# The first down block's low parts in a new order on VectorE, a hold on GpSimd's sums, and five products of zeros ahead of the first projection

## The chip, the cores and the metric

The kernel runs on one core of a Trainium2 chip. The metric is the device time of one execution in microseconds, from the first instruction to the last. Four engines compute: TensorE multiplies matrices into the eight banks of PSUM, VectorE and ScalarE read and write both SBUF and PSUM, and GpSimd works on SBUF alone. SyncE issues most DMAs. Each engine takes its own instructions strictly in the order in which they are written, and engines wait for one another by semaphores that count up.

## The reference

Two layers of a decoder trunk over 1024 tokens of width 1024. Layer 0 mixes tokens with gated linear attention and an RG-LRU, layer 1 with a gated delta rule. Each layer then attends to 256 memory tokens and applies an MLP. All in float32:

```python
for i in range(DEPTH):                      # DEPTH = 2
    hn = rms_norm(h, mix_pre_g[i])
    m = gla_lru_mixer(hn, ...) if i % 2 == 0 else gdn_mixer(hn, ...)
    h = h + rms_norm(m, mix_post_g[i])
    c = mem_cross_attn(rms_norm(h, xa_pre_g[i]), rms_norm(mem, xa_mem_g[i]), xa_w_q[i], xa_w_kv[i], xa_w_o[i])
    h = h + rms_norm(c, xa_post_g[i])
    f = sq_relu_mlp(rms_norm(h, mlp_pre_g[i]), mlp_w1[i], mlp_w2[i])
    h = h + rms_norm(f, mlp_post_g[i])

def sq_relu_mlp(h, w1, w2):                 # w1 1024 x 4096, w2 4096 x 1024
    return jnp.square(jax.nn.relu(h @ w1)) @ w2
```

## The kernel before

**Three products for one.** Every float32 operand of a matrix product is split into a high part (a copy rounded to fp32r, made by ScalarE) and a low part (the operand minus its high part, made by VectorE with one subtraction), and a product is three TensorE products of 128x128 by 128x512: high x high, high x low, low x high. Weights stream through four slots: SyncE loads a 128x1024 tile into `wraw`, ScalarE writes `whi`, VectorE writes `wlo` over `wraw`.

**The start.** The first projection of layer 0 (`first_pair`, L3397) multiplies the first two weight blocks with the eight tiles of x in the order in which they arrive. For each tile ScalarE makes the high part and squares x; VectorE makes the low part and adds the squares up. Ahead of the last tile stand two plain fp32 products with a matrix of ones (`first_stat`, L3415), which sum the squares over the partitions for the RMS norm. GpSimd sets two constant columns (L1093, L1094) and counts `cols_set`; ScalarE waits for both. GpSimd then spends the projection on sums of layer-1 weights (`presum`, L1099 to L1102), which SyncE loads and stores in a ring, between loads of weight tiles.

**The MLP by Strassen products.** Up and down projection use seven products instead of eight for 2x2 blocks (in Winograd's form). In the down projection the hidden units come in seven groups (`for i in range(MLP_G - 1)`), and in each group there are four output blocks a, b, c, d with seven products each. A product such as `a6` is one instruction group on TensorE: six products of 128x512, two k-tiles with three terms each. TensorE's order is

```python
PRODUCTS = ("a1 a5 b1 b5 a2 b2 a6 a3 b6 a7 b3 a4 b7 c1 c5 b4 c6 c2 c3 c7 d1 d5 c4 d6 d2 d7 d3 d4").split()
```

Products 1, 2 and 4 of a block take weight quarters as they are, products 3, 5, 6 and 7 take sums of them: S1 to S4 are made by GpSimd (`weight_sums`, L1045 to L1059, four 128x256 sums, S1 in place, counted by `x_sum`), the high parts `xh` of S2, S4 and S3 by ScalarE (`sums_hi`), their low parts `xl` by VectorE (`sums_lo`, `part_of_sums_lo`, counted by `x_split`). The hidden operands are B11, B21, B22, T1, T2, T3, T4. For group 0 they come back from DRAM raw, so ScalarE makes their high part (`raw_hi`, L1546) and VectorE their low part (`raw_lo`, L2578). The last hidden tile is staged for the later groups at the same time: GpSimd makes T's sums (`hidden_sums`, L1036 to L1042), ScalarE high parts (`part_hi`), VectorE low parts (`part_lo`, L2522), and SyncE stores them.

**Who waits for whom in group 0 of the down projection.** Products 1, 6, 7, 4 of a block accumulate in the same bank, and each partial sum is read out before the next product adds to it. So a7 waits until a6 was read, and a4 until a7 was read. In group 0, the products 1, 5, 6, 4 of a and b are read by ScalarE (`first_copy`, L1593, counted by `lam_exp`); VectorE stands in its order with a 128x1 memset that waits for this copy (L2615). All other products are read by VectorE: a copy (L2624) or an addition into `work` (L2626). `evac` counts them in order. ScalarE's order there, in the code of `mlp`:

```python
raw_hi("T4")
part_hi(PAIRS + 1, "T4")
first_copy("b5")
down_hi(0, 2)          # block c: whi (L1508), two high parts of sums (L1514)
first_copy("a6")
first_copy("b6")
```

The copy of b5 waits for the staged low part of B21. GpSimd's order is: hidden sums of the last tile, `down_prep(0, 2)` (block c), `down_prep(0, 3)` (block d), then the blocks of group 1. `down_prep(0, 2)` waits for its weights and for an up product; `down_prep(0, 3)` for the stores of the last staged tile. VectorE's order is written out by hand in L2628 to L2653: the low parts ahead of the loop, and inside it, behind the k-th read-out, further low parts and `down_lo(i, j)`, which splits a block and its sums.

Of the kernel before, what the change touches and what calls it, by code (L numbers as in the profile page):

```python
# [25 lines left out]
P = 128  # L26
# [11 lines left out]
LRU_C = 8.0  # L38
GLA_GATE_NORM = 16.0
GLA_RANK = 16  # L40
GDN_H = 8
XA_H = 4
XA_T = 2
# [272 lines left out]
def build(nc, xT, memT, wstream, lru_w, gk_w2, pvec_in, consts_in, masks_in, outT):  # L316
# [4 lines left out]
    with ExitStack() as ctx:  # L321
# [91 lines left out]
        def bank(b, n=1):  # L413
            return flat(ps[:, b:b + n, :])
# [175 lines left out]
        def all_out(op, layer, hp):  # L590

            return out_of_op(op), 16 * (len(EARLY) if op in EARLY else len(STAGED) - len(EARLY)) * (HIDDEN * layer + hp)
# [383 lines left out]
        def _(pool):  # L976
# [48 lines left out]
            def mlp(layer):  # L1025
# [18 lines left out]
                def weight_sums(blocks, parts, x):  # L1044

                    for n in blocks:
                        pool.wait_ge(w_in[plan.slot[n]], 16 * plan.nth[n])
                    a11, a12, a21, a22 = parts
                    w = x["w"]

                    def shaped(ap):
                        return pairs_of(ap) if w < HALF else ap
                    s2, s4, s3 = shaped(x["raw24"][:, 0:w]), shaped(x["raw24"][:, w:2 * w]), shaped(x["raw3"][:])
                    k3 = link.mark(tt(s3, a11, a21, ALU.subtract))  # L1054
                    tt(a21, a21, a22, ALU.add).then_inc(x_sum, 1)  # L1055
                    link.wait(k3)
                    k2 = link.mark(tt(s2, a22, s3, ALU.subtract))
                    link.wait(k2)
                    tt(s4, a12, s2, ALU.subtract).then_inc(x_sum, 1)  # L1059
# [4 lines left out]
                def down_prep(i, j):  # L1064
                    if i == 0 and j in (0, 2):
                        pool.wait_ge(unit_done, up_unit(layer, PAIRS - 2 + j // 2, "3") + 1)
                    if i == 0 and j == 3:
                        pool.wait_ge(*all_out("T2", layer, HIDDEN))
                    weight_sums((plan.at[f"mlp{layer}.d"][0] + MLP_T * i + j,), quarters(layer, None, i, j), sums_of(None, j))

                for hp in range(PAIRS):
# [18 lines left out]
                ppool[g].credit(pool)  # L1090
            gpool.credit(pool)
            gprep.credit(pool)
            nc.gpsimd.memset(one_col, 1.0).then_inc(cols_set, 1)  # L1093
            nc.gpsimd.memset(eps_col, EPS).then_inc(cols_set, 1)  # L1094
            for h in range(PRESUMS):
# [44 lines left out]
        def _(eng):  # L1140
# [970 lines left out]
            for s in (gexp, gqd, gev, gout, *pact, *fact, *oact):  # L2111
                s.credit(eng)
            eng.wait_ge(cols_in, 16)
            eng.wait_ge(cols_set, 2)
            first_part(0, False)
            for n in range(2):
                first_hi(n, 0)
# [22 lines left out]
        def _(eng):  # L2140
# [314 lines left out]
            def mlp(layer):  # L2455
# [171 lines left out]

                for i in range(MLP_G - 1):  # L2628
                    if i == 0:
                        part_of_sums_lo(prep_no(layer, None, 0, 1), sums_of(None, 1), 0, "24")  # L2630
                        raw_lo("B21")
                        raw_lo("T2")
                        raw_lo("B22")
                        part_lo(PAIRS + 1, "B21")
                        raw_lo("T3")
                        part_of_sums_lo(prep_no(layer, None, 0, 1), sums_of(None, 1), 1, "3")
                        part_lo(PAIRS + 1, "T13")
                    eng.wait_ge(evac, down_unit(layer, i, "a1"))
                    for k in range(len(PRODUCTS)):
                        add(i, k)  # L2640
                        if i == 0 and k == 3:
                            part_lo(PAIRS + 1, "T2")
                        if i == 0 and k == 5:
                            part_lo(PAIRS + 1, "T4")
                            raw_lo("T4")
                        if k == (5 if i else 9):
                            down_lo(i, 2)
                        if k == 14:
                            down_lo(i, 3)
                        if k == 19:  # L2650
                            down_lo(i + 1, 0)
                        if k == 23:
                            down_lo(i + 1, 1)  # L2653
# [691 lines left out]
        def _(eng):  # L3345
# [36 lines left out]
            def both_halves(n, u, i=0):  # L3382
# [11 lines left out]
                                      stop=kt == KT - 1 and (hl, xp) == terms[-1])  # L3394
                last.then_inc(unit_done, 1)

            def first_pair(n, u):  # L3397

                for kt in range(KT):
                    eng.wait_ge(act_ready, kt + 1)  # L3400
                    for j in range(2):
                        if kt in (0, KT // 2):
                            eng.wait_ge(w_split if kt else w_first_split, n + j + 1)
                        for hl, xp in ((0, 0), (0, 1), (1, 0)):
                            for e in range(2):
                                last = mm(out_of(u + j)[:, E[e]],
                                          (wlo if hl else whi)[plan.slot[n + j]][:, kt * P:(kt + 1) * P],
                                          act[:, kt, xp, E[e]], start=kt == hl == xp == 0,
                                          stop=kt == KT - 1 and hl == 1)
                        if kt == KT - 1:  # L3410
                            last.then_inc(unit_done, 1)
                    if kt == KT - 2:
                        first_stat()
# [806 lines left out]
```

## Time and profile before

| | us |
|---|---|
| median of 3 runs | 2982.55 (2981.35 to 2983.25) |
| the profiled execution | 2981.7 |
| its span | 2979.9 |
| TensorE busy, share | 98% |
| VectorE / ScalarE / GpSimd busy, share | 71% / 48% / 28% |
| granted clock, mean | 0.997 |

Shares are of the span. A matmul record shows a duration longer than its spacing, since products are pipelined: the spacing of starts is the measure. Layer 0's first down group begins near 1012 us, layer 1's some 1031 us later.

### The profile page before, as it was taken

How to read it: one execution, taken by the hardware profiler on the slowest of the kernel's cores; microseconds unless marked ns; L12 is line 12 of the kernel's file. 1: busy time of each engine (PE TensorE's matmuls, PEld its weight loads, DVE VectorE, ACT ScalarE, POOL GpSimd, SP SyncE). 2: the span in 40 equal slices, each digit the busy share in tenths (PEclk: the TensorE clock that was granted, in tenths of full speed). 3: DMA queues.
4: the chain of work that ended last, by engine and by line, in shares of the span. 5: the costliest groups of instructions: out<-in, count | busy, mean ns of one | idle time of the engine just before them, and what ended most of it. 6: DMA issues, size and time to landing. Idle time of an engine off the chain costs nothing.

```text
span 2979.9 us, 44588 instructions
## 1 busy us (share of the span) xinstructions
PE 2921.5 (98%) x16844; PEld 2403.1 (81%) x16844; DVE 2116.1 (71%) x2903; ACT 1441.4 (48%) x2651; POOL 840.6 (28%) x808
## 2 busy tenths in 40 slices
PE   8999999999999999999999999999999999999999
PEld 7788888887888778887788788878888788877887
DVE  8276638647788977778977666644764778897776
ACT  4435645336777712235433566644534677762222
POOL 4629300000566633330000112200000056663333
PEclk9999999999999999999999999999999999999999
DMA  6720341003566786533444323123101356677653
GB/s 216 254 92 22 108 126 50 29 29 113 205 254 249 272 327 247 212 114 131 154 146 149 104 61 121 49 71 113 43 29 34 136 201 249 250 296 289 254 205 135
DMA packets 198593, 457.35 MB, mean 153 GB/s; under 512 B 13808, under 2 KB 71440, under 8 KB 196496
## 3 DMA queue, kind: packets, MB, share of 16 engines
q1 hardware_dynamic: 159152, 414.34, 38.9%
q10 hardware_dynamic: 39264, 40.64, 4.0%
q8 instruction: 113, 1.85, 0.3%
q14 instruction: 64, 0.52, 0.1%
HBM read 304.97 MB, written 149.95 MB: 153 GB/s over the span
## 4 chain that ended last, share of the span: by engine, by line
PE 79%; DVE 12%; ACT 3%; issue 2%; DMA 2%; POOL 1%; SPq 0%; ACTq 0%; DVEq 0%; POOLq 0%
PE ps L3375 21%; PE ps L3607 10%; PE ps L3608 10%; PE ps L3609 10%; PE ps L3847 3%; PE ps L3848 3%; PE ps L3849 3%; PE ps L3882 2%; PE ps L3449 1%; DVE work L2177 1%; PE ps L3776 1%; PE ps L3392 1%; PE ps L4013 1%; DVE hres L2208 1%; PE ps L3996 1%
## 5 line engine op out<-in xcount | busy, mean ns | idle before, releaser
L3375 PE MATMUL ps<-act,whi 128*128 128x512 f32 x2384 | 747.8, 395 | 4.1 <-DVE act L2198 2.6
L3375 PEld LDWEIGHTS ps<-act,whi 128*128 128x128 f32 x2384 | 444.1, 188 | 110.6 <-issue 12.7
L3375 PE MATMUL ps<-act,wlo 128*128 128x512 f32 x1192 | 464.5, 390 | 0.0
L2161 DVE TENSOR_TENSOR wlo<-wraw,whi 128x1024 fp32r<-128x1024 f32 x253 | 319.1, 1263 | 188.6 <-ACT whi L1156 158.8
L1036 POOL TENSOR_TENSOR stagedf<-quads 128x1024 f32<-128x1024 f32 x28 | 73.8, 2635 | 1047.3 <-ACTq L1447 1047.3
L2626 DVE TENSOR_TENSOR work<-work,ps 128x512 f32<-128x512 f32 x360 | 239.6, 684 | 127.8 <-PE ps L3609 124.7
L1508 ACT ACTIVATE whi<-wraw 128x1024 fp32r<-128x1024 f32 x112 | 115.9, 1056 | 369.1 <-POOL wraw L1055 307.5
L3375 PEld LDWEIGHTS ps<-act,wlo 128*128 128x128 f32 x1192 | 223.7, 188 | 47.1
L3607 PE MATMUL ps<-act,whi 128*128 128x512 f32 x624 | 244.7, 392 | 7.1 <-DVE work L2626 4.0
L3609 PE MATMUL ps<-act,wlo 128*128 128x512 f32 x624 | 243.0, 389 | 0.0
L1156 ACT ACTIVATE whi<-wraw 128x1024 fp32r<-128x1024 f32 x124 | 130.4, 1057 | 151.6 <-DMA wraw<-wstream_dram 148.5
L3392 PE MATMUL ps<-act,whi 128*128 128x512 f32 x608 | 161.6, 392 | 0.9 <-DVE work L2960 0.8
L3608 PE MATMUL ps<-hresr,whi 128*128 128x512 f32 x416 | 161.9, 389 | 0.0
L3608 PE MATMUL ps<-act,whi 128*128 128x512 f32 x416 | 161.9, 389 | 0.0
L3607 PEld LDWEIGHTS ps<-act,whi 128*128 128x128 f32 x624 | 117.1, 188 | 37.4 <-DVE work L2626 9.6
L3609 PEld LDWEIGHTS ps<-act,wlo 128*128 128x128 f32 x624 | 117.1, 188 | 24.7
L3392 PEld LDWEIGHTS ps<-act,whi 128*128 128x128 f32 x608 | 114.8, 189 | 25.8 <-issue 2.1
L1054 POOL TENSOR_TENSOR xr_d<-wraw 128x256 f32<-128x256 f32 x56 | 50.8, 907 | 291.9 <-DMA wraw<-wstream_dram 276.3
L2522 DVE TENSOR_TENSOR staged<-stagedf,staged 128x512 fp32r<-128x512 f32 (+1 forms) x72 | 123.1, 1758 | 3.8 <-ACT staged L1471 3.5
L2238 DVE SCALAR_TENSOR_TENSOR work<-work,pvec 128x1023 f32<-128x1023 f32 (+2 forms) x84 | 111.9, 1332 | 3.0
L2177 DVE TENSOR_TENSOR work<-work,sq 128x512 f32<-128x512 f32 x83 | 57.3, 690 | 69.4 <-ACT sq L1184 69.2
L1126 POOL MEMSET work<- 128x1024 f32 x2 | 1.8, 952 | 358.4 <-PE ps L3849 358.4
(451 smaller groups left out, 7156.4 us busy)
## 6 DMA issues: line engine op xcount, KB each, us to landing
wraw<-wstream_dram SPq DMA_DIRECT2D x248, 512.0 KB, 3.6
hid_store<-staged SPq DMA_DIRECT2D x168, 512.0 KB, 3.3
act<-hid_store SPq DMA_DIRECT2D x36, 1024.0 KB, 10.8
hresr<-hid_store SPq DMA_DIRECT2D x56, 512.0 KB, 9.9
qkvz<-work ACTq DMA_DIRECT2D x32, 512.0 KB, 2.7
work<-qkvz ACTq DMA_DIRECT2D x64, 256.0 KB, 3.1
act<-hid_store SPq DMA_DIRECT2D x30, 512.0 KB, 10.9
presum<-wstream_dram SPq DMA_DIRECT2D x48, 256.0 KB, 4.0
```

What stands on the lines that cost most here:

```text
L1156: A(whi[s][:], wraw[s][:], ACT.Copy).then_inc(w_hi, 1)
L1508: A(whi[s][:], wraw[s][:], ACT.Copy).then_inc(w_hi, 1)
L2161: TT(wlo[s][:], wraw[s][:], whi[s][:].bitcast(F32), ALU.subtract).then_inc(w_split, 1)
L2238: ins = STT(out=out[:, back:], in0=x[:, 0:SEQ - back], scalar=w(3 - back), in1=out[:, back:], op0=ALU.mult, op1=ALU.add)
L2522: TT(stage_part(op, 1), src, stage_part(op, 0).bitcast(F32), ALU.subtract).then_inc(hid_ready, 1)
L2626: TT(uh(t, e), uh(t, e), out_of(uk), ALU.add).then_inc(evac, 1)
L3375: last = mm(out_of(u)[:, 0:width], (wlo if hl else whi)[s][:, at:at + P], rhs(kt, xp, e), start=kt == hl == xp == 0, stop=kt == kts - 1 an ...
L3392: last = mm(out_of(u)[:, E[e]], (wlo if hl else whi)[s][:, kt * P:(kt + 1) * P], act[:, kt, xp, E[e]], start=kt == hl == xp == 0, stop=kt ...
L3607: mm(out, wh, xh, start=first, stop=False, skip_group_check=more)
L3608: mm(out, wh, xl, start=False, stop=False, skip_group_check=more)
L3609: return mm(out, wl, xh, start=False, stop=end, skip_group_check=more)
L3847: mm(out_of(u), wh, xh, start=first, stop=False, skip_group_check=more)
```

## The change

Three edits.

1. GpSimd clears `sq` (128x512) ahead of the two columns, and TensorE multiplies its zeros five times, as fp32 products of 128x128 by 128x512 into bank 7, ahead of the first weight product. ScalarE's wait on `cols_set` goes up by one.
2. In group 0 of both layers' down projections VectorE's low parts are put in another order, and the next group's first block is split after the 17th read-out instead of the 19th.
3. GpSimd's sums of block c in group 0 wait until `x_split` says that VectorE has made both low parts of block b's sums.

```diff
@@ LRU_C = 8.0
+WARM = 5
@@ down_prep(i, j), GpSimd
                     if i == 0 and j == 3:
                         pool.wait_ge(*all_out("T2", layer, HIDDEN))
+                    if i == 0 and j == 2:
+                        pool.wait_ge(x_split, 2 * prep_no(layer, None, 0, 1) + 2)
                     weight_sums((plan.at[f"mlp{layer}.d"][0] + MLP_T * i + j,), quarters(layer, None, i, j), sums_of(None, j))
@@ GpSimd, start
+            nc.gpsimd.memset(sq[:], 0.0).then_inc(cols_set, 1)
             nc.gpsimd.memset(one_col, 1.0).then_inc(cols_set, 1)
@@ ScalarE, start
-            eng.wait_ge(cols_set, 2)
+            eng.wait_ge(cols_set, 3)
@@ VectorE, down projection
                     if i == 0:
-                        part_of_sums_lo(prep_no(layer, None, 0, 1), sums_of(None, 1), 0, "24")
                         raw_lo("B21")
                         raw_lo("T2")
                         raw_lo("B22")
+                        sums_lo(prep_no(layer, None, 0, 1), sums_of(None, 1))
+                        raw_lo("T3")
                         part_lo(PAIRS + 1, "B21")
-                        raw_lo("T3")
-                        part_of_sums_lo(prep_no(layer, None, 0, 1), sums_of(None, 1), 1, "3")
-                        part_lo(PAIRS + 1, "T13")
+                        raw_lo("T4")
                     eng.wait_ge(evac, down_unit(layer, i, "a1"))
                     for k in range(len(PRODUCTS)):
                         add(i, k)
                         if i == 0 and k == 3:
+                            part_lo(PAIRS + 1, "T13")
+                        if i == 0 and k == 5:
                             part_lo(PAIRS + 1, "T2")
-                        if i == 0 and k == 5:
                             part_lo(PAIRS + 1, "T4")
-                            raw_lo("T4")
                         if k == (5 if i else 9):
                             down_lo(i, 2)
                         if k == 14:
                             down_lo(i, 3)
-                        if k == 19:
+                        if k == (19 if i else 17):
                             down_lo(i + 1, 0)
@@ TensorE, start
+            def zeros():
+
+                eng.wait_ge(cols_set, 1)
+                for _ in range(WARM):
+                    mm(bank(7), sq[:, 0:P], sq[:], start=True, stop=True)
+
             def first_pair(n, u):
 
+                zeros()
```

VectorE at the head of layer 0's down projection, in the kernel before. `act` and `hresr` written by L2578 are the low parts of the hidden operands, in turn B21, T2, B22 and T3; `xl24_d1` and `xl3_d1` are the low parts of block b's sums; `staged` are the stored parts; `work` is where products are read out to:

```order
L2544 TENSOR_TENSOR xl24_d1_117<-xr24_d1_115,xh24_d1_113 128x512
L2578 TENSOR_TENSOR act_51<-act_51 128x2x512
L2578 TENSOR_TENSOR hresr_74<-hresr_74,tx_79 128x2x512
L2578 TENSOR_TENSOR act_51<-act_51 128x2x512
L2522 TENSOR_TENSOR staged1_82<-quads_80,staged1_82 128x512
L2578 TENSOR_TENSOR hresr_74<-hresr_74,act_51 128x2x512
L2544 TENSOR_TENSOR xl3_d1_118<-xr3_d1_116,xh3_d1_114 128x256
L2522 TENSOR_TENSOR staged0_81<-stagedf0_83,staged0_81 128x2x512
L2615 MEMSET small_67 128x1 x4
L2522 TENSOR_TENSOR staged1_82<-stagedf1_84,staged1_82 128x512
L2626 TENSOR_TENSOR work_69<-work_69,ps 128x512 x2
L2522 TENSOR_TENSOR staged1_82<-stagedf1_84,staged1_82 128x512
```

The same place in the changed kernel, where lines stand 4 further down:

```order
L2582 TENSOR_TENSOR act_51<-act_51 128x2x512
L2582 TENSOR_TENSOR hresr_74<-hresr_74,tx_79 128x2x512
L2582 TENSOR_TENSOR act_51<-act_51 128x2x512
L2548 TENSOR_TENSOR xl24_d1_117<-xr24_d1_115,xh24_d1_113 128x512
L2548 TENSOR_TENSOR xl3_d1_118<-xr3_d1_116,xh3_d1_114 128x256
L2582 TENSOR_TENSOR hresr_74<-hresr_74,act_51 128x2x512
L2526 TENSOR_TENSOR staged1_82<-quads_80,staged1_82 128x512
L2582 TENSOR_TENSOR hresr_74<-hresr_74,act_51 128x2x512
L2619 MEMSET small_67 128x1 x4
L2526 TENSOR_TENSOR staged0_81<-stagedf0_83,staged0_81 128x2x512
L2630 TENSOR_TENSOR work_69<-work_69,ps 128x512 x2
L2526 TENSOR_TENSOR staged1_82<-stagedf1_84,staged1_82 128x512 x2
```

The first part of block b's sums has moved behind B22, the second stands with it, T3 comes ahead of B21's staged part, and T4's low part, which was next behind the rows of the kernel before, has moved ahead of the memsets. The read-outs that follow (memset of a6, addition of a3, memset of b6, addition of a7) are the same in both.

VectorE further down in the same group, in the kernel before: the memset stands for b4, the copy reads c6, the three additions c2, c3 and c7, then the next group's first block (`wlo0`, `xl24_d0`, `xl3_d0`), then four copies of which the first reads d1:

```order
L2615 MEMSET small_67 128x1
L2624 COPY work_69<-ps 128x512
L2626 TENSOR_TENSOR work_69<-work_69,ps 128x512 x3
L2161 TENSOR_TENSOR wlo0_60<-wraw0_56,whi0_52 128x1024
L2544 TENSOR_TENSOR xl24_d0_111<-xr24_d0_109,xh24_d0_107 128x512
L2544 TENSOR_TENSOR xl3_d0_112<-xr3_d0_110,xh3_d0_108 128x256
L2624 COPY work_69<-ps 128x512 x4
```

And in the changed kernel:

```order
L2619 MEMSET small_67 128x1
L2628 COPY work_69<-ps 128x512
L2630 TENSOR_TENSOR work_69<-work_69,ps 128x512
L2165 TENSOR_TENSOR wlo0_60<-wraw0_56,whi0_52 128x1024
L2548 TENSOR_TENSOR xl24_d0_111<-xr24_d0_109,xh24_d0_107 128x512
L2548 TENSOR_TENSOR xl3_d0_112<-xr3_d0_110,xh3_d0_108 128x256
L2630 TENSOR_TENSOR work_69<-work_69,ps 128x512 x2
L2628 COPY work_69<-ps 128x512 x4
```

The three instructions of the next block stand ahead of the additions of c3 and c7. ScalarE's order is the same as before, GpSimd's too but for the memset, and SyncE's is the same.

## Rows read from the trace of the kernel before

**Rows 1.** The page, busy time of the engines.
```profile
PE 2921.5 (98%) x16844; PEld 2403.1 (81%) x16844; DVE 2116.1 (71%) x2903; ACT 1441.4 (48%) x2651; POOL 840.6 (28%) x808
```

**Rows 2.** Waits of TensorE: total us, times, longest.
```profile
PE ps L3607 <- DVE xl_d L2544: 3.6, 2, 1.8
...
PE ps L3607 <- DVE act L2578: 3.1, 2, 1.6
...
PE ps L3607 <- DVE work L2624: 1.8, 2, 1.1
```

**Rows 3.** Timeline of TensorE, layer 0's first down group: start, us, instruction, idle before.
```profile
1019.14 0.47 PE L3607 MATMUL ps<-act,whi 128*128 128x512 f32 x1 [1.55 <-DVE act L2578]
...
1026.67 0.50 PE L3607 MATMUL ps<-tx,xh_d 128*128 128x512 f32 x1 [1.81 <-DVE xl_d L2544]
...
1032.81 0.50 PE L3607 MATMUL ps<-act,whi 128*128 128x512 f32 x1 [1.76 <-DVE work L2626]
...
1050.52 0.47 PE L3607 MATMUL ps<-tx,xh_d 128*128 128x512 f32 x1 [1.10 <-DVE work L2624]
```

**Rows 4.** GpSimd's groups by form: busy us, mean ns, idle before.
```profile
L1105 POOL MEMSET lin<- 128x512 f32 x3 | 1.5, 528 | 43.8 <-DVE work L2811 43.8
```

**Rows 5.** Timeline of GpSimd at the start.
```profile
1.05 0.10 POOL L1093 MEMSET pvec<- 128x1 f32 x1 [0.60 <-POOLq L4211]
```

**Rows 6.** Timeline of TensorE at the start.
```profile
8.58 2.04 PE L3406 MATMUL ps<-act,whi 128*128 128x512 f32 x4 [8.58 <-DVE wlo L3314]
...
15.58 1.07 PE L3406 MATMUL ps<-act,whi 128*128 128x512 f32 x4
...
30.54 1.88 PE L3420 MATMUL ps<-work,consts 128*128 128x512 f32 x4
```

**Rows 7.** Windows: busy us of each engine, granted clock, DMA share, GB/s.
```profile
8.50:12.50 4.00, 3.92 (x9) 3.13 (x10) 3.37 (x4) 3.41 (x4) 0.00 (x0) 1.00 1.02 404
```

**Rows 8.** Timeline of VectorE at the start.
```profile
26.73 2.55 DVE L2229 TENSOR_TENSOR work<-work 128x1024 f32<-128x1024 f32 x2
```

**Rows 9.** The chain that ended last, 75 to 114 us.
```profile
105.88 4.88 DMA wraw<-wstream_dram
...
112.98 1.10 PE ps L3701 x2
```

**Rows 10.** Timeline of VectorE, layer 0's first down group.
```profile
1013.86 2.91 DVE L2544 TENSOR_TENSOR xl_d<-xr_d,xh_d 128x512 fp32r<-128x512 f32 x1
1016.69 2.31 DVE L2578 TENSOR_TENSOR act<-act 128x1024 fp32r<-128x1024 f32 x1
...
1021.16 1.77 DVE L2578 TENSOR_TENSOR act<-act 128x1024 fp32r<-128x1024 f32 x1
...
1031.45 1.30 DVE L2626 TENSOR_TENSOR work<-work,ps 128x512 f32<-128x512 f32 x2
```

**Rows 11.** Timeline of GpSimd in the same group.
```profile
1020.12 1.72 POOL L1054 TENSOR_TENSOR xr_d<-wraw 128x256 f32<-128x256 f32 x1
1021.79 1.73 POOL L1055 TENSOR_TENSOR wraw<-wraw 128x256 f32<-128x256 f32 x1
...
1024.75 1.58 POOL L1059 TENSOR_TENSOR xr_d<-wraw,xr_d 128x256 f32<-128x256 f32 x1
```

**Rows 12.** Timeline of ScalarE in the same group.
```profile
1021.64 1.06 ACT L1593 ACTIVATE work<-ps 128x512 f32<-128x512 f32 x2
...
1026.37 0.94 ACT L1514 ACTIVATE xh_d<-xr_d 128x512 fp32r<-128x512 f32 x2 [0.25 <-POOL xr_d L1059]
1027.21 0.58 ACT L1593 ACTIVATE work<-ps 128x512 f32<-128x512 f32 x1
```

**Rows 13.** Timeline of VectorE, later in the same group.
```profile
1045.98 1.77 DVE L2161 TENSOR_TENSOR wlo<-wraw,whi 128x1024 fp32r<-128x1024 f32 x1
...
1049.70 1.87 DVE L2624 COPY work<-ps 128x512 f32<-128x512 f32 x3
...
1053.92 1.02 DVE L2544 TENSOR_TENSOR xl_d<-xr_d,xh_d 128x512 fp32r<-128x512 f32 x2
```

## The prediction

> **What bounds the kernel now.** I read the page first: TensorE is busy for 98% of the span [rows 1]. Its waits come next. The reader is to see that the waits of L3607 (the Strassen products) come in pairs, one of a pair in each layer [rows 2]. A timeline of TensorE in layer 0 places four of them in one down block: 1.55 us ahead of a2, 1.81 ahead of b6, 1.76 ahead of a4, 1.10 ahead of d6 [rows 3]. The totals give layer 1 the same list (3.1 - 1.55, 3.6 - 1.81, 1.8 - 1.10; the third I take as equal at 1.76), so some 12.0 us in both layers. The change touches these waits and the kernel's start, where the first product waits for 8.58 us [rows 6]. In the two down blocks the wait that ends last is what counts, and there VectorE, GpSimd and ScalarE run a race for TensorE's next operand or bank. Outside them TensorE is the bound, and a microsecond won is kept, unless a chain that TensorE doesn't pace stands close behind it.
>
> **The start: five products of zeros.** GpSimd first clears `sq`: 0.53 us, as the 128x512 memset of [rows 4], from where it now sets its first column, 1.05 us [rows 5]. So TensorE can start near 1.7. A fp32 product is two records: the pair of statistics products has 4 records in 1.88 us, 0.43 us apart [rows 6]. The granted clock reads 1.00 from 8.5 to 12.5 us [rows 7], yet the first four products start 0.43 us apart ((2.04 - 0.76) / 3), which for 512 columns is the level of 1.2 GHz; from 15.58 it is (1.07 - 0.39) / 3 = 0.227 us, the level of 2.4 GHz [rows 6]. So a slow phase is there, though the clock row doesn't show it: the 18 products before 15.58 cost 7.00 - 18 x 0.227 = 2.9 us too much. The ten records of the zeros take 6.9 us, from 1.7 to 8.6, if some six are slow (0.86 each) and four fast. If all are slow they end at 10.3.
> Not all of the 2.9 us comes back. The statistics products need VectorE's last sum of squares, which ends at 26.73 + 2.55 = 29.28 [rows 8], in a chain that starts from the DMAs of x and not from TensorE. They start at 30.54 now [rows 6], so they can move to 29.4 at most: 1.1 us. Behind them stands a second chain. TensorE's wait at 112.98 ends with a weight tile that landed at 110.76, at the end of a long ring of GpSimd sums and DMAs [rows 9]. TensorE sets that ring off, but in its first part it takes turns with VectorE, which I expect not to move. If the ring doesn't move, all 1.1 us is lost there; if it moves whole, all is kept. I take 0.6, with 0 and 1.1 as ends.
> The Trainium skill (TensorE: Matmul & The Clock Gate, What's actually happening) holds that the array is throttled by default and that activity lifts this; it says nothing of the data. By it zeros serve as well as weights, and the sum stands; were they not to count, the sum would be that of rival C. This trace shows the slow phase but has no product of zeros to tell.
>
> **The down block: what the new order wins.** Low parts on VectorE now come as B21, T2, B22, the sums of block b, T3. I replay layer 0 (times less 1000). Where both want it, VectorE and GpSimd take turns: GpSimd's sum from 20.12 ends at 21.84, VectorE's low part from 21.16 ends 1.09 later at 22.93, and GpSimd's from 21.79 ends 0.59 after that [rows 10, 11]. So a 128x1024 part takes 1.09 once its turn comes and a 128x512 part half, 0.55; a GpSimd sum of 128x256 takes 0.59 and one of 128x512 twice that.
> - B21 no longer stands behind block b's part, which ended at 16.77 [rows 10]. It has that part's turn, from 16.77 - 0.55 = 16.2, and ends at 17.3 instead of 19.0. a2 is due at 19.14 - 1.55 = 17.6: the first wait goes, with 0.2 us to spare.
> - T2 ends near 19.5, a sum of GpSimd later (a6 is due at 20.3). B22 takes its turn after GpSimd's last hidden sum and ends near 21.8. a3 needs ScalarE's copy of a5, the first of two from 21.64 [rows 12], and starts near 22.4 (0.7 late).
> - GpSimd is idle by then, so the sums of block b cost 1.02 as the undisturbed pair of [rows 13] and are there at 22.75; b6 starts at 23.75. The second wait goes (1.81).
>
> **What the hold costs.** GpSimd may begin the sums of block c at 22.8 instead of 20.12. What matters is who waits for them. ScalarE's order is unchanged: copy of b5, the three high parts of c, and only then the copy of a6. Product a7 adds into the bank of a6, so it waits for that copy. Until now GpSimd's last sum ended at 26.33 [rows 11], the high parts from 26.37 at 27.31, the copy at 27.79 [rows 12], and a7 started near 28.1 (26.67 + 6 x 0.227) behind b6, so this chain was hidden by a few tenths. Now the four sums take turns with T3, B21's staged part, T4 and T13 on VectorE: the sums end at 24.4, 25.55, 27.2 and 28.9. High parts 28.95 to 29.85, the copy to 30.4, a7 at 30.5. It is due at 25.1: a new wait of 5.4 us. a4 has a7 and b3 ahead of it (2 x 1.36), so it starts at 33.25, against 32.81 [rows 3].
> A second count says the same. a4 also needs VectorE's add of a7, which ended at 31.45 + 1.30 = 32.75 [rows 10]. Ahead of this add VectorE has exactly the same instructions in both orders, and GpSimd as many sums to take turns with. So a4 can't start much before 31.7. For a4 the ends are 31.7 and 34.9 (rival B); I take 33.25: three waits (5.12 us) become one of about the same size, and each layer loses 0.44 there.
> The Trainium skill (SBUF — State Buffer, SBUF: two separate sides) calls the shared pair of ports an exclusive lock, held for a whole instruction when VectorE has two SBUF inputs. The rows of the turns agree to 0.1 us. By that rule a hold moves the turns and removes none; if the ports were shared as bandwidth, an early finish on GpSimd could be bought, which is rival A.
>
> **What c3 and c7 behind the next block's parts bring.** VectorE splits block a of the next group from 45.98, and the copy of d1 comes only after it, at 49.70 [rows 13]; d6 waits for this copy (1.10, in layer 1 0.7). With the split two adds earlier it begins near 43.9, ends near 46.5, and then come c3 and c7 (to 47.8) and d1 (to 48.4). By 1.36 us per product from a4, c4 needs c7's add at 48.2 and d6 needs d1's copy at 49.6: both are met by a few tenths. Gain 1.10 and 0.7. Were GpSimd to take turns through the whole split (3.7 us as now), c4 would stand about 1 us and the gain is near zero. I take it whole.
> What is left is covered. The zeros' bank 7 has no other use until long after, and the clearing of `sq` delays the columns that ScalarE needs to 1.7 us, when it still has no x. The staged parts are stored up to 1 us later; GpSimd's sums of block d wait for these stores, but VectorE comes to block d only after the copy of c5, near 39.
>
> **Sum.** Against the profiled execution, 2981.7 us: -0.6 (start), -1.10 + 0.44 (layer 0), -0.70 + 0.44 (layer 1) = -1.4, so 2980.3. It ran 0.85 us below the median of 2982.55; against that, 2981.1, or 2981 in round numbers.
>
> **Rivals.**
> - A, the waits just go. For it: each is named in the trace, and each has its edit. It needs a6's copy by 24.9, that is GpSimd done by 23.4. Gain 12.0 + 1.1: 2969.5; half of it, 2976. Against it: GpSimd starts later than now, and VectorE has as much to do. Chance 0.14.
> - B, slower: the copy of a6 behind the held sums. If the low parts take 2.3 us each as B21 does now [rows 10], the hold ends at 23.2; four sums at 1.73 [rows 11] end at 30.4, a7 starts at 32.2, a4 at 34.9: 2.1 lost per layer. With the start's gain absorbed and d6's 1.8 kept: +2.4, 2985.0. It decides from a4 later than 34.0 (1.2 past the present 32.81, twice, eats 1.8 + 0.6). Chance 0.14.
> - C, the zeros don't lift the clock. They end at 10.3, 1.7 us after the first product could start, and this is as slow as now: -0.6 turns into +1.7, 2983.3. For it: only that no row shows zeros. Chance 0.08.
> - My forecast, one wait exchanged for another: 0.64, by itself 2979 to 2983.
>
> **Numbers.** About 0.2% (6 us) is what a measurement can tell from no change. Faster by more needs half of A or all: 0.13. Slower by more needs B at its worst plus something unseen: 0.06. Same: 0.81. The range runs from 2976 (half of A) to 2985 (B).
>
> **What would show it.** Right: products start 0.23 us apart from the first weight on, and the statistics products start near 29.4. In the down block no wait ahead of a2, b6, a4 and d6, but one of some 5 us ahead of a7, released by ScalarE's copy (L1593 before), itself behind high parts that waited for GpSimd. Wrong: no wait ahead of a7 (A); a4 later than 34.0 (B); products 0.43 us apart after the zeros (C); the wait at 112.98 grown to 2.9 us would mean that nothing of the start was kept.

## The result, and the profile after

| | before | changed |
|---|---|---|
| median of 22 runs each, interleaved, us | 2983.65 (2980.2 to 2986.7) | 2987.77 (2982.49 to 2994.05) |
| ratio, 95% interval | | 1.0015 (1.0009 to 1.0020) |
| the profiled execution, us | 2981.7 | 2983.24 |
| its mean granted clock | 0.997 | 0.996 |
| mean granted clock over all timed runs | 0.9963 | 0.9941 |

The change costs 4.1 us. I had forecast a gain of 1.4. The two profiled executions lie only 1.5 us apart, so they show where time goes and not how large the loss is. On the page of the changed kernel TensorE's busy time, 2928.6 us against 2921.5 [rows 1], has grown by about what the ten records of zeros take (7.4 us); the loss doesn't stand out there:

```profile
PE 2928.6 (98%) x16854; PEld 2407.1 (81%) x16854; DVE 2109.3 (71%) x2903; ACT 1440.6 (48%) x2651; POOL 839.2 (28%) x809
```

TensorE's waits (total us, times, longest) answer to [rows 2]. The two releasers of a2 and b6, L2578 and L2544 before, are gone from the list. The first line is new; it holds one wait of 5.49 us in each layer, ahead of a7:

```profile
PE ps L3617 <- ACT work L1597: 11.1, 3, 5.5
...
PE ps L3617 <- DVE work L2630: 3.7, 5, 1.1
...
PE ps L3404 <- POOL pvec L1098: 2.0, 1, 2.0
...
PE ps L3711 <- ACT lin L1668: 0.4, 1, 0.4
```

The start of TensorE's timeline answers to [rows 6]. Behind the zeros the four products of a row take 1.09 us, (1.09 - 0.39) / 3 = 0.23 us apart, where they took 2.04 before:

```profile
2.02 7.37 PE L3404 MATMUL ps<-sq 128*128 128x512 f32 x10 [2.02 <-POOL pvec L1098]
9.04 1.27 PE L3416 MATMUL ps<-act,whi 128*128 128x512 f32 x4
...
10.60 1.09 PE L3416 MATMUL ps<-act,whi 128*128 128x512 f32 x4
```

TensorE in group 0 of layer 0, which answers to [rows 3]. The row of 1020.72 is the last product of b6, that of 1026.59 the first of a7, that of 1031.82 the first of a4:

```profile
1020.72 0.39 PE L3619 MATMUL ps<-tx,xl_d 128*128 128x512 f32 x1
1026.59 0.80 PE L3617 MATMUL ps<-act,xh_d 128*128 128x512 f32 x1 [5.49 <-ACT work L1597]
...
1027.61 0.63 PE L3619 MATMUL ps<-act,xl_d 128*128 128x512 f32 x1
1028.04 0.63 PE L3617 MATMUL ps<-act,xh_d 128*128 128x512 f32 x1
...
1031.82 0.40 PE L3617 MATMUL ps<-act,whi 128*128 128x512 f32 x1
1032.05 0.40 PE L3618 MATMUL ps<-hresr,whi 128*128 128x512 f32 x1
```

Two things are to be seen. No wait stands ahead of a2, b6, a4 or d6 in this group. And the twelve products of a7 and b3 start 0.43 us apart, those behind them 0.23. The windows (length, busy us of PE, PEld, DVE, ACT and POOL, granted clock, DMA share, GB/s) say why: TensorE is at the level of 1.2 GHz.

```profile
1020.00:1026.50 6.50, 1.10 (x5) 0.56 (x3) 6.50 (x12) 3.09 (x7) 5.00 (x4) 0.88 0.38 158
1026.60:1028.00 1.40, 1.40 (x3) 1.16 (x4) 1.00 (x4) 0.43 (x1) 0.00 (x0) 0.50 1.03 418
1028.00:1030.00 2.00, 2.00 (x6) 1.59 (x5) 0.44 (x1) 0.00 (x0) 0.00 (x0) 0.50 1.03 422
1030.00:1032.00 2.00, 2.00 (x6) 1.59 (x6) 2.00 (x3) 0.00 (x0) 1.06 (x2) 0.57 0.17 70
1032.00:1034.00 2.00, 2.00 (x10) 1.61 (x10) 2.00 (x3) 0.60 (x2) 2.00 (x2) 1.00 0.00 0
```

The same stretch of the kernel before, with its waits of 1.81 and 1.76 us, keeps the level of 2.4 GHz:

```profile
1026.60:1028.00 1.40, 1.33 (x6) 1.11 (x7) 1.40 (x7) 1.19 (x3) 0.00 (x0) 1.00 0.00 0
1028.00:1030.00 2.00, 2.00 (x11) 1.65 (x10) 2.00 (x4) 0.60 (x1) 0.00 (x0) 1.00 0.72 295
1030.00:1032.00 2.00, 1.04 (x5) 0.54 (x3) 1.88 (x4) 0.00 (x0) 0.00 (x0) 1.00 1.03 424
```

Layer 1 repeats it: a7 behind an idle time of 5.49 us, and the lower clock after it.

```profile
2661.08 0.80 PE L3617 MATMUL ps<-act,xh_d 128*128 128x512 f32 x1 [5.49 <-ACT work L1597]
```
```profile
2661.00:2665.00 4.00, 3.92 (x9) 3.14 (x10) 2.05 (x6) 0.51 (x2) 0.00 (x0) 0.50 0.98 399
2665.00:2667.00 2.00, 2.00 (x7) 1.51 (x6) 2.00 (x3) 0.00 (x0) 1.60 (x2) 0.57 0.00 0
```

I laid the two timelines of TensorE side by side, product by product in the same order. The starts after the change, minus those before, in us:

| at (time before) | difference | what happened since the row above |
|---|---|---|
| 30.5, statistics products | -0.8 | zeros |
| 113.0 | -2.2 | the wait of 1.83 there shrank to 0.4 |
| 130.4 | -3.6 | before had a half-clock stretch here, the changed profile none |
| 1019.1, a2 | -5.5 | wait of 1.55 gone |
| 1026.7, b6 | -7.1 | wait of 1.81 gone |
| 1028.2, a7 | -1.6 | new wait of 5.49 |
| 1032.8, a4 | -1.0 | lower clock +2.4, wait of 1.76 gone |
| 1050.5, d6 | -2.4 | wait of 1.10 gone |
| 1089.9 and 1109.3 | -1.9, -1.3 | groups 1 and 2, below |
| 2657.7 to 2661.7, layer 1 | -3.7 to +4.2 | new wait and lower clock |
| 2663.9 to 2681.2, a4 and d6 of layer 1 | +2.5 to +1.7 | waits of 1.75 and 0.72 gone |
| end | +1.5 | |

The step of 130.4 is a matter of which run was profiled. Short half-clock stretches turn up in every trace here, also where no wait is long (that of the kernel before, at 127 us, has no wait above 0.3 us in the 10 us ahead of it), and the middle of the program shifts by some 1.5 us either way for the same reason.

### The profile page after: what moved, and what is told of

Its sections match the earlier page's. It is cut to its first block, busy times and chain, and to the rows that moved or that the text cites. A ratio compares the mean times of both kernels' runs of the same rounds, so it can differ in the third digit from the quotient of the medians.

```text
span 2981.4 us, 44609 instructions
## 1 busy us (share of the span) xinstructions
PE 2928.6 (98%) x16854; PEld 2407.1 (81%) x16854; DVE 2109.3 (71%) x2903; ACT 1440.6 (48%) x2651; POOL 839.2 (28%) x809
## 4 chain that ended last, share of the span: by engine, by line
PE 78%; DVE 12%; ACT 3%; issue 3%; POOL 2%; DMA 2%; ACTq 0%; SPq 0%; DVEq 0%; POOLq 0%
PE ps L3378 21%; PE ps L3617 11%; PE ps L3618 11%; PE ps L3619 11%; PE ps L3892 2%; PE ps L3857 2%; PE ps L3858 2%; PE ps L3859 2%; PE ps L3459 1%; DVE work L2181 1%; PE ps L3786 1%; PE ps L4023 1%; DVE hres L2212 1%; PE ps L3746 1%; DVE work L2197 1%
## 5 line engine op out<-in xcount | busy, mean ns | idle before, releaser
L2630 DVE TENSOR_TENSOR work<-work,ps 128x512 f32<-128x512 f32 x360 | 239.4, 683 | 133.4 <-PE ps L3619 130.4
L1160 ACT ACTIVATE whi<-wraw 128x1024 fp32r<-128x1024 f32 x124 | 130.4, 1057 | 155.3 <-DMA wraw<-wstream_dram 152.1
L3617 PEld LDWEIGHTS ps<-act,whi 128*128 128x128 f32 x624 | 117.4, 188 | 30.4 <-DVE work L2630 5.7
## 6 DMA issues: line engine op xcount, KB each, us to landing
act<-hid_store SPq DMA_DIRECT2D x36, 1024.0 KB, 10.9
```

The lines of the kernel that those rows point to most:

```text
L1160: A(whi[s][:], wraw[s][:], ACT.Copy).then_inc(w_hi, 1)
L2630: TT(uh(t, e), uh(t, e), out_of(uk), ALU.add).then_inc(evac, 1)
L3617: mm(out, wh, xh, start=first, stop=False, skip_group_check=more)
```

## The experiments

Each was timed in 5 rounds beside the kernel before on the same chip. There were three chips: one for e1, e2, e4 and e5, one for e3, e6, e9 and e10, one for e11 to e13. So a comparison across these groups is best made by what each differs from its own reference. None of them changes what is computed; where products are added, nothing reads their bank.

**One part alone: the zeros (e1).** On the kernel before:

```diff
+            nc.gpsimd.memset(sq[:], 0.0).then_inc(cols_set, 1)
-            eng.wait_ge(cols_set, 2)
+            eng.wait_ge(cols_set, 3)
+                zeros()
```

> The kernel before with the five zero products and the clearing of sq alone. If the start's gain is real and carries (the changed kernel's trace stands 0.8 us ahead behind the statistics products and 2.2 us ahead behind the wait at 112.98), it is 2 us faster than before in the median, about 2981.5, and the waits ahead of a2, b6, a4 and d6 are those of before. Rival: the zeros are what made the changed kernel slower (by the clock or later in the chain): then it is 2 to 4 us slower, near 2987.

Measured: 2980.83 (2978.53 to 2985.02) against 2982.85, ratio 0.9995 (0.9986 to 1.0004). The median lies where the sum has it, but the interval holds "no change" too. The trace stands ahead of that of before step by step: -0.96 us at the statistics products and -1.42 at 113.0. All four waits of [rows 3] stand, and three have their size:

```profile
1018.31 0.47 PE L3616 MATMUL ps<-act,whi 128*128 128x512 f32 x1 [1.55 <-DVE act L2580]
1025.82 0.50 PE L3616 MATMUL ps<-tx,xh_d 128*128 128x512 f32 x1 [1.81 <-DVE xl_d L2546]
1031.95 0.50 PE L3616 MATMUL ps<-act,whi 128*128 128x512 f32 x1 [1.74 <-DVE work L2628]
```

So the zeros aren't what made the kernel slower. (d6's wait is 0.55 us here.)

**The other parts alone (e2).** The changed kernel without those lines:

> The changed kernel without the zeros: the new order and the hold alone. Theory: the wait of 5.5 us ahead of a7 in each layer, and the half clock behind it (some 12 products at 0.43 us apart, 2.4 us), are all here, so it is slower than the changed kernel by what the zeros brought, 2 us: 5 to 7 us slower than before, near 2989.5, and its runs spread over 10 us as those of the changed kernel do. Rival (zeros to blame): it is as fast as before, 2983.

Measured: 2987.65 (2983.31 to 2991.32) against 2982.85, ratio 1.0016 (1.0007 to 1.0025). The whole loss is here, 4.8 us, a little under the 5 to 7 expected. The wait ahead of a7 stands, 5.29 us in this trace's layer 0. Beside the changed kernel (2987.77) the zeros show no gain, so their 2 us isn't a settled figure.

**Without the hold (e3).** The changed kernel less

```diff
-                    if i == 0 and j == 2:
-                        pool.wait_ge(x_split, 2 * prep_no(layer, None, 0, 1) + 2)
```

> The changed kernel with GpSimd's hold taken out: the sums of block c start as early as before. Theory: the hold delays the copy of a6 by some 2.5 us, so a7's wait falls from 5.5 to about 2.5 us, b6 gets a wait of about 0.6 back (VectorE's sums of b take turns with GpSimd again), and a4, which needs VectorE's add of a7, gets one of 1.5 to 3: no wait is long enough to drop the clock each time, and the median is 3 to 5 us below the changed kernel's, 2983 to 2984.5. Rival: the order alone is to blame and the hold is innocent: 2987, with a7 still waiting 5 us.

Measured: 2983.67 (2980.22 to 2989.61) against 2982.69, ratio 1.0003 (0.9994 to 1.0011). It takes back 4 us of the loss, but a7 waits for 4.0 us where I expected 2.5, and behind that the clock falls too:

```profile
1028.01 0.79 PE L3615 MATMUL ps<-act,xh_d 128*128 128x512 f32 x1 [4.04 <-ACT work L1595]
```
```profile
1028.00:1030.00 2.00, 2.00 (x5) 1.61 (x6) 1.88 (x5) 0.44 (x1) 0.00 (x0) 0.50 0.92 377
```

The clock fell behind a7 in both layers, which I hadn't expected either. So the new order of the low parts alone makes most of the wait: TensorE comes to a7 three microseconds earlier, while the copy of a6 still stands behind GpSimd's sums and ScalarE's high parts. The hold adds 1.5 us and lengthens the slow stretch.

**The clock or the wait (e5).** This is the experiment that tells the two apart. On the changed kernel TensorE fills the idle time ahead of a7 with products into bank 3:

```diff
+                    if i == 0:   # ahead of a7's wait
+                        (wh, _), rhs = weights("A11", 0, None, 0, 1), moving("B11", 0, 0)
+                        for _ in range(22):
+                            mm(bank(3), wh, rhs, start=True, stop=True)
```

> The changed kernel with 22 more products per layer ahead of a7, of block b's weights with B11 into a bank that nothing reads, so that TensorE works through 5.0 us of the 5.5 us for which it waits. The results are untouched. Theory: the wait's end doesn't move, but the products behind it start 0.23 us apart, so each layer wins back the 2.4 us of half clock and the runs lie closer together: some 5 us faster than the changed kernel in the median, 2982 to 2984. Rival: the clock costs nothing here since VectorE is the bound behind a7: the same as the changed kernel, 2987 to 2988.

Measured: 2980.39 (2978.82 to 2984.36) against 2982.85, ratio 0.9988 (0.9979 to 0.9997); 7.4 us below the changed kernel by the medians, 6.6 if each is set against its own reference (-2.5 and +4.1), and more than the 5 expected. a7 begins no earlier by this edit, since the copy that it waits for is the same: the fill ends at 1031.43 and 0.56 us are still idle. What differs is the clock behind it, 1.00 in the window, and products 0.23 us apart:

```profile
1026.28 5.15 PE L3667 MATMUL ps<-act,whi 128*128 128x512 f32 x22
1031.99 0.50 PE L3618 MATMUL ps<-act,xh_d 128*128 128x512 f32 x1 [0.56 <-ACT work L1598]
1032.33 0.40 PE L3619 MATMUL ps<-hresr,xh_d 128*128 128x512 f32 x1
```
```profile
1026.00:1036.00 10.00, 9.44 (x42) 7.48 (x42) 9.29 (x17) 3.56 (x6) 4.40 (x3) 1.00 0.64 262
```

The mean clock over all runs rises from 0.9941 to 0.9968. With the wait left and the clock behind it kept, the loss is gone: the clock is its cause.

**Shortening the wait (e4).** ScalarE copies a6 ahead of block c's high parts, and the hold stays:

```diff
                     first_copy("b5")
+                    first_copy("a6")
                     down_hi(0, 2)
-                    first_copy("a6")
```

> The changed kernel with one line of ScalarE moved: the copy of a6 ahead of the three high parts of block c. The hold stays. Theory: a7's wait falls from 5.5 us to under 1.5, the clock stays at 2.4 GHz, and a4 is released by VectorE's add of a7 near where the add stands ready now; each layer gains 3 to 5 us against the changed kernel: 2978 to 2981, 3 to 5 faster than before. Rival: the wait only moves (a7 or a4 waits 5 us for VectorE instead): the same as the changed kernel, 2987.

Measured: 2983.88 (2978.23 to 2988.42) against 2982.85, ratio 1.0007 (0.9998 to 1.0016). 4 us better than the changed kernel, but not better than the kernel before: a miss. a7's wait shrinks to 1.24 us, and the idle time turns up again at a4, for VectorE's add of a7:

```profile
1028.27 0.50 PE L3617 MATMUL ps<-act,xh_d 128*128 128x512 f32 x1 [1.24 <-ACT work L1597]
1034.33 0.50 PE L3617 MATMUL ps<-act,whi 128*128 128x512 f32 x1 [3.04 <-DVE work L2630]
```
```profile
1034.00:1036.00 2.00, 1.67 (x5) 1.34 (x6) 2.00 (x4) 0.00 (x0) 0.00 (x0) 0.76 1.02 418
```

**Shortening it and keeping the clock (e10).** e4 with 12 such products ahead of a4:

> Copy of a6 first, the hold kept, and 12 more products (2.7 us) ahead of a4, where TensorE waits 3.0 us, into a bank that nothing reads. Theory: the wait's end stays, but the clock no longer falls behind a4 (it fell there in layers 0 and 1 in the variant without them, for 3.4 us of the trace each): mean clock up from 0.995 to 0.997 and 3 us faster, 2980 to 2981.5. Rival: 3 us of idle time don't drop the clock, the stretches are random: the same as without, 2984.

Measured: 2979.17 (2977.7 to 2982.25) against 2982.69, ratio 0.9991 (0.9982 to 0.9999), 4.7 us below e4 by the medians, as much by the references, and a little better than expected. It has the lowest median of this study; the intervals of e1, e5 and e11 overlap its own.

```profile
1027.56 2.88 PE L3667 MATMUL ps<-act,whi 128*128 128x512 f32 x12
1030.76 0.50 PE L3618 MATMUL ps<-act,whi 128*128 128x512 f32 x1 [0.33 <-DVE work L2631]
```
```profile
1032.00:1034.00 2.00, 2.00 (x10) 1.65 (x9) 1.56 (x5) 0.60 (x1) 0.68 (x1) 1.00 0.59 178
```

**Without hold, with the early copy (e6), and that with the waits filled (e12).** e6 is e4 less the two lines of e3. e12 adds 8 products ahead of a7 and 5 ahead of a4.

> Copy of a6 ahead of block c's high parts, and no hold. Theory (VectorE has the same work ahead of its add of a7 whatever the order): a7 waits about 1 us, a4 about 3 us for that add, as with the hold, so it is within 1.5 us of the variant with the copy first and the hold, 2983 to 2985. Rival (the hold costs by itself): 2 to 3 us faster than that, near 2981.

Measured: 2983.47 (2979.54 to 2986.52) against 2982.69, ratio 1.0001 (0.9991 to 1.0010). Now a7 waits for T3's low part and a4 for the add of a7:

```profile
1028.11 0.50 PE L3615 MATMUL ps<-act,xh_d 128*128 128x512 f32 x1 [2.25 <-DVE hresr L2580]
1033.12 0.50 PE L3615 MATMUL ps<-act,whi 128*128 128x512 f32 x1 [1.98 <-DVE work L2628]
```

Waits of about 2 us were long enough here: in layer 0 the clock fell behind a4, in layer 1 behind a7 (2.27 us).

```profile
1034.00:1036.00 2.00, 2.00 (x7) 1.58 (x6) 1.74 (x5) 0.60 (x1) 0.35 (x1) 0.60 0.57 227
```

> Copy of a6 first, no hold, and products that nothing reads ahead of a7 (8, 1.8 us of its 2.25 us wait) and ahead of a4 (5, 1.1 us of its 2.0 us). Theory: without them the clock fell behind these waits in both layers for 3.4 us of the trace; with them it holds, so it is some 3 us faster than without, 2979.5 to 2981.5. Rival: waits of 2 us are short enough, and the stretches come from elsewhere: 2983.5, as without.

Measured: 2983.03 (2977.13 to 2985.27) against 2983.78, ratio 0.9998 (0.9988 to 1.0007). A miss: 0.4 us below e6, though its profile has no half-clock stretch in the group and the mean clock rose from 0.9954 to 0.9963. Filling helps much where waits were of 3 and 5.5 us (e10, e5), and not measurably here. The expectation counted both slow stretches of e6, but that of layer 1 cost little: it took up time that a4 would have waited for VectorE's add, and a4's wait there is 0.43 us instead of 1.98. And in e12's trace a half-clock stretch stands in group 2 instead, behind a wait of 2.22 us. Why e12 stays above e10, whose trace has the same (2.07 us), is open.

**The split behind the 17th read-out (e9, e11).** e9 is e1 with the split moved in every group, e11 in group 0 only, as the change has it:

```diff
-                        if k == 19:
+                        if k == 17:                 # e9
+                        if k == (19 if i else 17):  # e11
```

> The kernel before with the zeros, and with the next group's first block split behind the 17th read-out in every group, not in group 0 alone. Theory: d6's wait goes in group 0 (1.1 and 0.7 us) and isn't given back in group 1, since there too d1's copy stands ahead of nothing; 1.5 to 3 us faster than with the zeros alone, about 2978.5 to 2979.5. Rival: the additions of c3 and c7, now late, hold c7 or c4 in the later groups: 0 to 2 us slower than with the zeros alone, 2981 to 2983.

Measured: 2999.40 (2995.04 to 3004.98) against 2982.69, ratio 1.0053 (1.0038 to 1.0067), 18.6 us above e1. Both the expectation and its rival (at most 2983) missed by far. In later groups c4 waits for c7's add, now behind the split. TensorE's waits on the adds rise from 5.4 us in all (e1) to 21.6, among them c4's of 2.31 us in group 1:

```profile
PE ps L3616 <- DVE work L2628: 21.6, 21, 2.9
```
```profile
1087.44 0.50 PE L3616 MATMUL ps<-act,whi 128*128 128x512 f32 x1 [2.31 <-DVE work L2628]
```

> The kernel before with the zeros and with the next group's block split behind the 17th read-out in group 0 alone, as the changed kernel has it, but with the old order of low parts and no hold. Theory: d6's wait in group 0 goes (0.6 us each layer in the trace with zeros alone), and about as much comes back as waits in group 1 and 2 (in the changed kernel 1.1 and 0.5 us came back in layer 0): within 1 us of the zeros alone, 2980 to 2982. Rival: it is kept, 2979.

Measured: 2980.78 (2978.71 to 2985.27) against 2983.78, ratio 0.9989 (0.9981 to 0.9998). The median is that of e1 (2980.83). In the trace TensorE gains 1.3 us at d6 against the products ahead of it (-1.29 to -2.55), of which e1 shows 0.5 without this edit (-0.86 to -1.40), and the gain is still there at 1089.9 (-2.65). For what it is worth in a run, 1 us, the timing can't tell.

This trace holds one thing more. In these two groups e11 has only the old waits, all under 2 us, and in layer 1 the clock fell behind b6's, which is as long as in the kernel before:

```profile
2658.07 0.50 PE L3616 MATMUL ps<-tx,xh_d 128*128 128x512 f32 x1 [1.83 <-DVE xl_d L2546]
```
```profile
2660.00:2662.00 2.00, 2.00 (x6) 1.61 (x5) 2.00 (x4) 0.40 (x1) 0.00 (x0) 0.50 1.03 422
```

It cost nothing: the slow products took up the time for which a4 waits otherwise, and a4 waits hardly at all here.

**The changed kernel again (e13).**

> The changed kernel itself beside the two others, on their chip. It should give 2987 to 2988.5, with a mean clock near 0.994 against 0.997 of the kernel with zeros alone: 3 in a thousand of 2985 us are 9 us of lost clock, of which 6 to 7 us should be seen as time. If it comes out within 2 us of the others, the difference was the chip's and not the kernel's.

Measured: 2987.67 (2982.88 to 2990.18) against 2983.78, ratio 1.0012 (1.0004 to 1.0021). The loss repeats, and so does its picture:

```profile
1029.67 0.79 PE L3617 MATMUL ps<-act,xh_d 128*128 128x512 f32 x1 [5.48 <-ACT work L1597]
```
```profile
1030.00:1032.00 2.00, 2.00 (x6) 1.52 (x6) 0.70 (x2) 0.11 (x1) 0.00 (x0) 0.50 1.03 422
1032.00:1034.00 2.00, 2.00 (x6) 1.61 (x5) 1.36 (x2) 0.00 (x0) 0.00 (x0) 0.50 0.73 297
```

## Why the prediction failed

**The chain that the forecast named was right, to a tenth or two.** To compare with its replay I add 3.82 us to the changed kernel's times, since TensorE came to the group that much earlier, and leave out the 1000. GpSimd's sums, which it had beginning at 22.8 and ending at 28.9, begin at 19.02 + 3.82 = 22.84 and end at 23.50 + 1.59 + 3.82 = 28.91. GpSimd:

```profile
1019.02 1.60 POOL L1055 TENSOR_TENSOR xr_d<-wraw 128x256 f32<-128x256 f32 x1 [2.15 <-issue]
...
1023.50 1.59 POOL L1060 TENSOR_TENSOR xr_d<-wraw,xr_d 128x256 f32<-128x256 f32 x1
```

ScalarE waits for them and only then makes the high parts and the copy of a6:

```profile
1025.12 0.94 ACT L1518 ACTIVATE xh_d<-xr_d 128x512 fp32r<-128x512 f32 x2 [2.27 <-POOL xr_d L1060]
1025.96 1.07 ACT L1597 ACTIVATE work<-ps 128x512 f32<-128x512 f32 x2
```

a7 starts at 26.59 + 3.82 = 30.41 (forecast 30.5), behind 5.49 us of idle time (forecast 5.4). The waits of a2, b6 and d6 went, as forecast.

**The step that failed** is the sentence "three waits become one of about the same size, and each layer loses 0.44 there". It counts idle time as if it were all alike. In the trace of before, three waits of 1.55, 1.81 and 1.76 us left the clock at 2.4 GHz; one of 5.49 dropped it to 1.2. Behind it the twelve products of a7 and b3 start 0.427 us apart instead of 0.227: 12 x 0.20 = 2.4 us per layer, 4.8 in both, a term that the sum didn't have. With it, a4 came 2.83 us later against the entry of the group (-0.99 from -3.82), not 0.44. In the forecast's own frame that is 35.6, past the point (34.0) from which it said that the kernel gets slower. So rival B's size came true by another road: it had a4 at 34.9 by slow sums on GpSimd, and it was the clock. VectorE's add of a7 shows that nothing else was late. It stands idle for 1.84 us, waiting for slow products:

```profile
1029.56 0.69 DVE L2630 TENSOR_TENSOR work<-work,ps 128x512 f32<-128x512 f32 x1 [1.84 <-PE ps L3619]
```

I had the means to see it: the forecast's own first part reads 0.43 us against 0.23 at the start and calls it the clock, and then prices only the start. The Trainium skill (TensorE: Matmul & The Clock Gate, HAM oscillation — how this bites in real kernels) says that long idle gaps between matmuls throttle the array again, so that the next products run at half the clock. By it the sum would have had this term. The trace agrees, with 0.50 in the window of 1026.60 to 1028.00; the page's case is a DMA wait in a loop, here it is one wait for a bank in a kernel that is busy for 98%.

**Size of the term in the median.** e5 recovers 7.4 us by the medians, 6.6 by the references; the profile shows 4.8. The mean granted clock over the runs goes from 0.9941 to 0.9968, and 0.0027 of 2980 us is 8.0 us of work at full clock. The changed profile has 6.8 us at half clock in each of the two groups, which lowers its mean clock by 0.0023, and some of it falls into the wait and costs nothing. So these two stretches are most of the difference in clock. The 2 us or so that are left lie within the intervals of the timings; whether slow stretches elsewhere add to it wasn't settled. The changed kernel's mean clock came out at 0.9948 when it was run again (e13), and e3 has the same 0.9948 at 4 us less, so the mean clock alone doesn't give the time.

**The balance**, each beside its own reference: zeros -2.0 (e1), the order, the hold and the split with the clock kept -0.5 more (e5 is 2.5 below the kernel before), the clock +6.6. That this adds up to 4.1 proves nothing, since the last term is the difference of two of the timings. The independent count is the forecast's -1.4 (its terms in fact add up to -1.5, and rival B's four sums to 30.1 and not 30.4, which takes 0.6 us off B) with 4.8 us of slow products from the profile: +3.4, against 4.1 measured.

**The zeros.** Right: they lift the clock as weights do (rival C is out), and products start 0.23 us apart from the second on. The zeros themselves ran from 2.02 to 9.38 (forecast 1.7 to 8.6), since seven of the ten records were slow and not six, and the first weight product came 0.46 us later than before. The statistics products moved by 0.8 to 1.0 us (forecast at most 1.1). Of this I took 0.6 as kept; in the traces the wait at 113.0 ends 1.4 to 2.2 us earlier. Part of this may be scatter: the trace of e2, without zeros, stands at -0.4 and +0.4 at the same two places. Why the ring of GpSimd and DMAs moved more than TensorE did wasn't looked into.

**The hold.** The forecast put a7's wait down to the held sums. e3 shows that 4.0 of the 5.5 us are there without it. That the chain behind GpSimd was "hidden by a few tenths" was read rightly; what I missed is that removing the waits of a2 and b6 alone uncovers it by 3.4 us. Rival A, the waits just going, falls for the same reason, and e4 and e6 show its limit: with the copy early, VectorE's work ahead of the add of a7 is next, and a4 waits for 2 to 3 us.

The Trainium skill (SBUF — State Buffer, SBUF: two separate sides) speaks of an exclusive lock. The forecast used it to say that the hold would move the turns of VectorE and GpSimd and remove none. The trace bears this out: held or not, a sum of 128x256 mostly takes 1.6 to 1.7 us beside VectorE (1.60 and 1.59 above, 1.58 to 1.73 in [rows 11]), and one of the four takes 1.2 in both orders.

**d6.** The wait went, but not all of the gain stayed. In groups 1 and 2 TensorE now waits:

```profile
1088.02 0.47 PE L3617 MATMUL ps<-tx,xh_d 128*128 128x512 f32 x1 [1.12 <-DVE work L2630]
```
```profile
1108.05 0.50 PE L3617 MATMUL ps<-act,xh_d 128*128 128x512 f32 x1 [0.46 <-DVE work L2630]
```

In the kernel before, one wait of 0.46 us stood in that stretch. d6's 1.1 in layer 0 was given back by the end of group 2. "I take it whole" was too much for the changed kernel, while in e11, with the old order of low parts, most stays.

**The chances.** I took 6 us as what a measurement can tell. 22 runs of each told 4.1 apart from nothing, so "same" at 0.81 was too coarse a class. Of the overshoot beyond 2985, 1.1 us is the reference, which came out at 2983.65 in 22 runs and 2982.55 in the 3 ahead of the forecast; even against the latter +4.1 is past the +2.4 of B. I had asked for a loss beyond B to have "something unseen" and looked for it only among the engines' races. A change that gathers scattered waits into a long one is a case in which the clock has to be among the rivals.

## What to carry to other kernels

Idle time on the bounding engine isn't worth only its length: here a wait of 5.5 us cost 2.4 us more in slower products behind it, one of 3.0 some 1.7 us (3.4 us at half clock in e4). Waits of about 2 us were followed by the lower clock in some traces and not in others, and those of 1.6 to 1.8 almost never. What a slow stretch costs also hangs on what stands behind it: where the next product would have waited anyway (e11, e6 in layer 1), it cost nearly nothing. So before moving waits together, look at the granted clock and at the spacing of starts behind every long wait in the trace. Where a long wait can't be removed, a run of products that nothing reads, ended a little before the operand comes, kept the clock and was worth some 7 us (e5) and 4.7 us (e10) in two layers; ahead of waits of about 2 us it brought nothing that could be measured (e12).

## What the runs showed of the hardware

- Products of zeros lift TensorE's clock: behind ten records of them the products start 0.23 us apart, without them 0.43.
- A fp32 product of 512 columns shows as two records. Those of the statistics products are 0.4 us apart at the level of 2.4 GHz (four in 1.95 us at 29.72), twice the spacing of the others; the zeros' ten take 7.37 us, the first seven at the lower level, some 0.85 us each.
- Behind idle times of 5.5, 4.0, 3.0 and 2.0 us ahead of a7 or a4 (e13, e3, e4, e6), the granted clock was 0.50, 0.50, 0.76 and 0.60 in the next 2 us window; behind 1.8 us it was 1.00 in the kernel before and 0.50 in layer 1 of e11.
- I counted TensorE's waits of 1.5 us and more in the 13 traces, between 20 and 2950 us. Of the 10 of 3.0 us or more all had a half-clock stretch with them or within 5 us after them, of the 36 of 1.8 to 2.9 us 15 had one, of the 18 shorter ones none. One wait of 1.9 us, near 1432, stands in all 13 traces, and in 6 of them the lower clock follows (0.50 in e13 from 1434.2 to 1437.2, 1.00 at that place in the kernel before). So its length alone doesn't decide. Slow stretches also stand where waits are shorter: somewhere between 1680 and 1704 us in every trace, among waits of 0.5 to 1.2 us.
- Runs of one kernel differ in granted clock, and those with less of it are longer: the changed kernel's run at 0.992 took 2994.05 us, those at 0.996 took 2983.24 to 2984.68. Its 22 runs span 11.6 us, e10's 12 span 4.6; but the 33 of the kernel before beside e1 span 10.9 at a mean clock of 0.9963, so a high mean clock doesn't make the spread small.
